# Query blocks of the attention from last to first, and the bias transposes behind the first two score blocks

## What is computed

```
q_blocks = moveaxis(q.reshape(bsz, n_blk, Q_BLOCK, MLA_HEADS, QK_HEAD), 1, 0)
def attend(args):
    qb, i = args
    q_chunk = (i * Q_BLOCK + arange(Q_BLOCK)) // CHUNK
    allowed = k_chunk[None, :] <= q_chunk[:, None]
    s = einsum("bqhd,bkhd->bhqk", qb, k) * scale
    s = where(allowed[None, None], s, neg)
    p = softmax(s, axis=-1)
    return einsum("bhqk,bkhd->bqhd", p, v)
o = lax.map(attend, (q_blocks, arange(n_blk)))
...
h = h + concatenate([conv_out, attn_out], axis=-1) @ w_o[l]
h = h + moe_ffn(rmsnorm(h, norm_ffn[l]), w_router[l], ...)
```

## Time and profile before

| | us |
|---|---|
| median of 3 runs | 2291.48 |
| lowest and highest | 2290.32 and 2299.23 |
| time of the profiled execution | 2284.88 |
| its span | 2283.0 |
| first stage, to the last transposes of queries and keys | 0 to 363.7 |
| second stage | 363.7 to 711 |
| third stage | 711 to 2283 |

### The profile page before, as it was taken

One profiled execution on the slowest core, in us unless ns is written; L12 is line 12 of the kernel. 1 busy time (PEld: TensorE's weight loads), 2 busy tenths in 40 slices (PEclk: granted clock), 3 DMA queues, 4 the chain that ended last, 5 costly groups with the idle time before them and its releaser, 6 DMA issues.

```text
span 2283.0 us, 42195 instructions
## 1 busy us (share of the span) xinstructions
PE 2123.9 (93%) x15622; PEld 1923.6 (84%) x15623; DVE 730.0 (32%) x1930; ACT 404.3 (18%) x1018; POOL 558.1 (24%) x637
## 2 busy tenths in 40 slices
PE   6999997899984899999999999999999999999992
PEld 5888885455544899999999999999999999999992
DVE  0222222333323233433233332333333333343331
ACT  1221212323211111111111111111111111111110
POOL 1122221010022223223322332222232322323321
PEclk9999998999986999999999999999999999999996
DMA  7000004212104889999998999999999989999997
GB/s 271 10 18 9 9 1 147 56 28 56 29 19 143 263 261 323 315 291 290 296 294 273 310 296 289 299 289 288 271 302 311 315 262 273 315 316 314 301 289 85
DMA packets 305781, 486.70 MB, mean 213 GB/s; under 512 B 106786, under 2 KB 128162, under 8 KB 305698
## 3 DMA queue, kind: packets, MB, share of 16 engines
q1 hardware_dynamic: 249394, 441.14, 59.2%
q0 software_dynamic: 33120, 44.91, 9.4%
q10 hardware_dynamic: 23232, 0.18, 0.6%
HBM read 454.81 MB, written 35.84 MB: 215 GB/s over the span
## 4 chain that ended last, share of the span: by engine, by line
PE 88%; DVE 3%; issue 3%; SPq 1%; ACT 1%; DMA 1%; POOL 1%; ACTq 0%; DVEq 0%; POOLq 0%
PE psum L975 41%; PE psum L991 22%; PE psum L798 7%; PE psum L940 5%; PE psum L811 2%; PE psum L889 1%; PE psum L846 1%; PE psum L814 1%; PE psum L888 1%; PE psum L923 1%; PE psum L852 1%; PE psum L906 1%; PE psum L952 1%; DMA area<-in_x 1%; DVE area L1289 1%
## 5 line engine op out<-in xcount | busy, mean ns | idle before, releaser
L975 PE MATMUL psum<-area 128*128 128x128 f32 (+2 forms) x8192 | 994.4, 284 | 40.9 <-issue 23.1
L975 PEld LDWEIGHTS psum<-area 128*128 128x128 f32 x8192 | 985.7, 192 | 46.4 <-issue 46.3
L991 PE MATMUL psum<-area 128*128 128x128 f32 (+2 forms) x4096 | 502.8, 284 | 1.6
L991 PEld LDWEIGHTS psum<-area 128*128 128x128 f32 x4096 | 491.2, 191 | 10.7 <-DVE area L1289 9.9
L1270 DVE TENSOR_SCALAR area<-psum,area 128x160 f32<-128x160 f32 x256 | 86.5, 379 | 628.5 <-PE psum L975 628.5
L575 POOL DMA_INDIRECT sum_rows<-area x165 | 261.8, 1587 | 67.3 <-issue 40.2
L737 ACT ACTIVATE area<-area 128x320 f32<-128x320 f32 x128 | 60.2, 470 | 754.2 <-DVE area L1270 754.2
L798 PEld LDWEIGHTS psum<-area 128*128 128x128 f32 x1536 | 176.2, 194 | 3.8 <-issue 3.3
L798 PE MATMUL psum<-area 128*128 128x128 f32 x1536 | 177.6, 277 | 0.0
L565 POOL DMA_INDIRECT area<-normed_rows,area x165 | 160.5, 972 | 62.1 <-issue 61.8
L560 POOL TENSOR_TENSOR area<-area 128x5 uint32<-128x5 uint32 x33 | 6.2, 189 | 644.4 <-DVE area L1255 607.1
(11 more groups left out here) (187 smaller groups left out, 1273.4 us busy)
## 6 DMA issues: line engine op xcount, KB each, us to landing
area<-in_w_gate_up SPq DMA_DIRECT2D x256, 1024.0 KB, 6.3
area<-in_w_down SPq DMA_DIRECT2D x128, 1024.0 KB, 6.9
area<-in_x SPq DMA_DIRECT2D x16, 512.0 KB, 4.0
area<-in_w_in SPq DMA_DIRECT2D x1, 4096.0 KB, 12.9
area<-in_w_o SPq DMA_DIRECT2D x1, 4096.0 KB, 13.7
sum_rows<-area SPq DMA_DIRECT2D x32, 128.0 KB, 2.7
normed_rows<-area SPq DMA_DIRECT2D x8, 512.0 KB, 2.8
out<-sum_rows SPq DMA_DIRECT2D x4, 1024.0 KB, 13.8
```

The costliest lines, as they stand in the source:

```text
L975: ins = mm(dst, w_gu[piece][:, k, c * P:(c + 1) * P], xT[:, PART * s + k, 0:width], start=(s == 0 and k == 0 and c % 2 == 0), stop=(s == 1 ...
L991: ins = mm(bank[4 + d // 3][:, (d % 3) * SLOTS:(d % 3) * SLOTS + width], w_dn[q][:, kk, d * P:(d + 1) * P], actT[:, 2 * q + kk, 0:width], ...
```

## The change

A table ORDER holds the query blocks from 7 to 0. Wherever a step used its position as the query block it now uses ORDER of the position: the length of the scores, the number of key tiles in TP and PV, the slices of queries, convolution output, x rows and of the two DRAM arrays that take h and the normalized rows. The token numbers in the constants follow the same order. The ranks inside an expert are now given from the last token block to the first, so each expert's list has its tokens in another order. The list of steps itself is the same. The order in which positions use the second transpose bank changes with the number of key tiles.

Separately, the bias transposes on TensorE and the VectorE copies behind them are moved to unit n = 2, ahead of S 2, and the wait for the copies (bank 6 is PV's output) to PV 0.

```diff
+ORDER = list(range(NT - 1, -1, -1))
...
-        "tokens": Q * (p + P * np.arange(NT, dtype=np.float32)[None, :]),
+        "tokens": Q * (p + P * np.array(ORDER, np.float32)[None, :]),
...
-            if kind == "HT" or (kind == "TP" and n // HEADS >= 4):
+            if kind == "HT" or (kind == "TP" and ORDER[n // HEADS] >= 4):
...
-                sp.dma_start(h_sb[i], x_rows[i]).then_inc(hx_in[i], 16)
+                sp.dma_start(h_sb[i], x_rows[ORDER[i]]).then_inc(hx_in[i], 16)
...
-            pe.wait_ge(bias_in, 16 * 3)
             pe.wait_ge(qT_ready, 3 * NT)
             pe.wait_ge(kT_ready, NT)
-            for c in range(2 * NC):
-                tr(bank[7][:, c * E:(c + 1) * E], bias_rows[0:E, c * P:(c + 1) * P], ident[0:E, 0:E])
...
-            pe.wait_ge(bias_ready, 2)
             pe.wait_ge(conv_done, NT)
+
+            def turn_biases():
+
+                pe.wait_ge(bias_in, 16 * 3)
+                for c in range(2 * NC):
+                    tr(bank[7][:, c * E:(c + 1) * E], bias_rows[0:E, c * P:(c + 1) * P], ident[0:E, 0:E])
...
                 if kind == "S":
-                    i, h = n // HEADS, n % HEADS
+                    i, h = ORDER[n // HEADS], n % HEADS
+                    if n == 2:
+                        turn_biases()
...
                 if kind == "PV":
-                    i, h = n // HEADS, n % HEADS
+                    i, h = ORDER[n // HEADS], n % HEADS
                     pe.wait_ge(turn_a_read, use_a[("TP", n)])
+                    if n == 0:
+                        pe.wait_ge(bias_ready, 2)
...
-                        lhs = convT[:, k, i * P:(i + 1) * P] if k < NF else attnT[:, k - NF, :]
+                        lhs = convT[:, k, ORDER[i] * P:(ORDER[i] + 1) * P] if k < NF else attnT[:, k - NF, :]
```

More of the change, by code:

```diff
@@ L443, in _ @@
             for i in range(NT):
-                b = i % 2
+                b, rows_at = i % 2, slice(ORDER[i] * P, ORDER[i] * P + P)
                 sp.wait_ge(h_ready, 2 * (i + 1))
@@ L447, in _ @@
                 for q in range(Q):
-                    sp.dma_start(acc_by_chunk[i * P:(i + 1) * P, :, q, :], h_chunks[:, :, q, :]).then_inc(h_out, 16)
+                    sp.dma_start(acc_by_chunk[rows_at, :, q, :], h_chunks[:, :, q, :]).then_inc(h_out, 16)
                 sp.wait_ge(hf_ready, i + 1)
-                sp.dma_start(hf_dram[i * P:(i + 1) * P, :], hf).then_inc(hf_out, 16)
+                sp.dma_start(hf_dram[rows_at, :], hf).then_inc(hf_out, 16)
                 if i + 2 < NT:
                     sp.wait_ge(h_out, 16 * Q * (i + 1))
-                    sp.dma_start(h_sb[b], x_rows[i + 2]).then_inc(hx_in[b], 16)
+                    sp.dma_start(h_sb[b], x_rows[ORDER[i + 2]]).then_inc(hx_in[b], 16)
             sp.wait_ge(tables_ready, 1)
@@ L681, in _ @@
                 if kind == "S":
-                    i = n // HEADS
-                    L = (i + 1) * P
+                    L = (ORDER[n // HEADS] + 1) * P
                     act.wait_ge(s_max, n + 1)
@@ L692, in _ @@
                 if kind == "TP":
-                    i = n // HEADS
+                    i = ORDER[n // HEADS]
                     act.wait_ge(turn_a, use_a[(kind, n)])
@@ L858, in _ @@
             turn_qk(NT - 1)
-            pe.wait_ge(bias_in, 16 * 3)
             pe.wait_ge(qT_ready, 3 * NT)
             pe.wait_ge(kT_ready, NT)
-            for c in range(2 * NC):
-                tr(bank[7][:, c * E:(c + 1) * E], bias_rows[0:E, c * P:(c + 1) * P], ident[0:E, 0:E])
-            for c in range(KD):
-                ins = tr(bank[6][:, c * E:(c + 1) * E], bias_rows[0:E, 2 * FF + c * P:2 * FF + (c + 1) * P], ident[0:E, 0:E])
-            ins.then_inc(bias_turned, 1)
-            pe.wait_ge(bias_ready, 2)
-            pe.wait_ge(conv_done, NT)
+            pe.wait_ge(conv_done, NT)
+            def turn_biases():
+                pe.wait_ge(bias_in, 16 * 3)
+                for c in range(2 * NC):
+                    tr(bank[7][:, c * E:(c + 1) * E], bias_rows[0:E, c * P:(c + 1) * P], ident[0:E, 0:E])
+                for c in range(KD):
+                    ins = tr(bank[6][:, c * E:(c + 1) * E], bias_rows[0:E, 2 * FF + c * P:2 * FF + (c + 1) * P], ident[0:E, 0:E])
+                ins.then_inc(bias_turned, 1)
             def rank_of(n, dst):
@@ L897, in _ @@
                         pe.wait_ge(exp_done, n + 1)
-                        src = [prob[n % 2][:, k * P:(k + 1) * P] for k in range(n // HEADS + 1)]
+                        src = [prob[n % 2][:, k * P:(k + 1) * P] for k in range(ORDER[n // HEADS] + 1)]
                     if kind == "OT":
@@ L1118, in _ @@
             nm = attn_stat[:, 120:128]
-            dve.wait_ge(bias_turned, 1)
-            V.tensor_copy(bguT, bank[7].rearrange("p (c e) -> p c e", e=E)).then_inc(bias_ready, 1)
-            V.tensor_copy(bdT, bank[6][:, 0:KD * E].rearrange("p (c e) -> p c e", e=E)).then_inc(bias_ready, 1)
-            V.memset(cums[:, 0, :], 0.0)
-            V.tensor_copy(entries[:, :, :, 0], last(K["tokens"], TOPK))
             def places(n):
@@ L1134, in _ @@
             for kind, n in steps:
+                if kind == "S" and n == 2:
+                    dve.wait_ge(bias_turned, 1)
+                    V.tensor_copy(bguT, bank[7].rearrange("p (c e) -> p c e", e=E)).then_inc(bias_ready, 1)
+                    V.tensor_copy(bdT, bank[6][:, 0:KD * E].rearrange("p (c e) -> p c e", e=E)).then_inc(bias_ready, 1)
+                    V.memset(cums[:, 0, :], 0.0)
+                    V.tensor_copy(entries[:, :, :, 0], last(K["tokens"], TOPK))
                 if kind == "S":
-                    i = n // HEADS
-                    L = (i + 1) * P
+                    L = (ORDER[n // HEADS] + 1) * P
                     sc = psum[:, (n % 2) * 1024:(n % 2) * 1024 + L]
@@ L1147, in _ @@
                     if kind == "TP":
-                        m = n // HEADS + 1 - 4
+                        m = ORDER[n // HEADS] + 1 - 4
                         if n >= 2:
```

## The result

| | before | after |
|---|---|---|
| median of the runs | 2291.92 us | 2305.06 us |
| lowest to highest (runs) | 2290.32 to 2299.23 (6) | 2301.41 to 2306.74 (6) |
| the profiled execution | 2284.88 us | 2306.74 us |
| its mean granted clock | 0.966 | 0.958 |

The ratio is 1.0051 (95% interval 1.0036 to 1.0066): the changed kernel is slower by 0.5%, 11.7 us (the two medians differ by 13.1). The forecast was +4.7. The time lies in the range, near its upper end, where the prediction gave 0.16 to being slower by more than 0.5%. The sign is the forecast's; the size is not.

What follows compares the result with a forecast made beforehand. TensorE, busy for 93% of the span, was taken to bound the kernel. The terms -6.5 + 1.4 - 1.7 + 7.2 - 0.5 + 4.8 gave +4.7 us on the median of 2291.48: 2296 us, range 2283 to 2307.

Steps and rivals of the forecast that it cites:

- S 0 earlier: Start of the second stage: the first scores start at about 364.95 instead of 371.43, -6.5 us.
- Bias transposes: Ahead of S 2: the transposes move but do not vanish, +1.4 us at full clock, +2.75 if still half.
- First position at low clock: Behind S 0's start: half-clock loss of 2.4 us instead of 4.1, so -1.7 us (between 0 and -2.4).
- Waits: Behind the odd output projections: TensorE waits longer where short units give less cover, +7.2 us in all, +5.4 from first PVs.
- second waits: At the next PV behind those projections: 1.2 us for one tile, 0.65 for two, 0.2 for three; +1.1 us.
- Small terms: HT's copy, PV 30 and the work behind the last unit: together -0.5 us.
- Clock in the short positions: Last, short positions: half-clock stretches lose 9.9 us instead of 5.1, so +4.8 us (0 to +14).
- rival B: Last three positions: clock falls early and stays low into the next projection, +17.3 us, 2309 us; chance 0.13.
- A: Short positions: clock falls no more often than before, term zero, sum -0.1, 2291 us; chance 0.27.
- C: Second stage: waits behind projections do not grow, only S 0's early start counts, -8, 2283 us; chance 0.06.
- D: Third stage: expert lists in another order change gathers and scatters, 0 with 4 us to either side; chance 0.06.

Runs made afterwards that it cites:

- e3: The changed kernel with the scores' second matmul over 128 rows instead of 64 in units 0 to 3; 2329.49 us, not comparable; S 0 to the experts 365.9 us.
- e11: The changed kernel with the scores' first matmul over 64 of its 128 rows in units 0 to 3; total not comparable, clock back 8 us behind S 0.
- e4: The changed kernel plus seven unread matmuls in TensorE's wait ahead of the last transposes; 2278.1 us, ratio 0.9939.
- e12: The kernel before, unchanged, profiled a second time; 2292.0 us.
- e10: e9 plus 1, 2, 2 and 3 unread matmuls in the waits behind the odd projections of positions 4 to 7; 2265.57 us, ratio 0.9889.
- e1: The kernel before with only the bias transposes moved to unit 2, blocks in their old order; 2283.33 us, ratio 0.9954.
- e7: The changed kernel with the loads of w_o and all behind it held until the fourth unit's exponential is done; 2302.98 us (one run).
- e5: e1 plus the seven unread matmuls ahead of the last transposes; 2281.9 us, ratio 0.9957.
- e6: The kernel before plus the seven unread matmuls ahead of the last transposes; 2283.32 us, ratio 0.9964.
- e2: The kernel before with only the block order reversed, bias transposes still ahead of S 0; 2303.81 us, ratio 1.0044.
- e8: e5 plus unread matmuls ahead of the last PV, the last position's HT, the ranks and the experts; 2266.22 us, ratio 0.9888.
- e9: e8 with the blocks from last to first and 4 instead of 3 unread matmuls ahead of PV 31; 2271.6 us, ratio 0.9924.

## Why the prediction was right or wrong

1. **S 0 earlier: right.** L785 to S 0 took 4.06 us instead of 10.57, -6.5 as forecast. It started at 363.76, not 364.95, since L785 came 1.2 earlier in that execution.
2. **Bias transposes: the other price.** They ran from 381.69 to 384.4, 2.7 us, which the prediction had named for a half clock. I took the full clock. PV 0 did not wait for the copies, as forecast.
3. **First position at low clock: wrong, and the largest miss.** The step that failed is "In the only stretch like that, the even projection behind the last unit, the clock rose 3.3 us after its start". I took a loss of 2.4 us from it, with ends of 1.7 and 4.1; it was 16.9. The projection has dense 512-column matmuls, but all over 128 rows; the scores alternate 128 and 64. (Whether that is why they differ is supported by e3 and e11, not settled.) The projection was not the only stretch to read, either: the scores of before, at 0.50 for 8.2 us, were the same matmuls but for their length, and I had no ground to make their loss the upper end. e3 and e4 confirm that this is where the time went: they take 15.6 and 15.8 us off the second stage. Against the execution of the prediction the term is +12.8; against e12 it is +5.0; the forecast had -1.7.
4. **Waits: right for the first PV; the second ones were covered by the low clock.** For 6 to 1 tiles the first waits were 0 (0.41 on VectorE instead), 0.65, 1.59, 2.13, 2.56 and 2.98: 9.9 against the 10.4 of the forecast. The second waits did not come: the PVs at 576.45, 612.93 and 643.38 start with no wait. Behind 609 and 640 the clock was at half in between, and the slower PV, TP and S covered the chain; the cost was then in the clock. At full clock, in e10, these two waits are 0.56 and 1.08, where 0.65 and 1.2 had been worked out. The wait of 0.77 that three tiles had before is gone for another reason, and ScalarE's timeline of after shows it:

```profile
575.92 0.48 ACT L698 ACTIVATE area<-psum 128x384 f32<-128x384 f32 x1
```

This copy ends at 576.40, just ahead of PV at 576.45. From the first PV to the end of the chain it is now 3.0 us, not 3.3, since ScalarE's longer copy (0.58 us instead of 0.36) lets the first PV start later while VectorE works on. And the first PV is that of a block with four tiles, 0.99 us instead of 0.55, which covers the rest. All waits of the stage are +6.5 against e12, where +7.2 was forecast.
5. **Small terms: right.** HT's group went from 2.7 to 2.4 us. PV 30 waited 0.37. From TP 31 at 669.79 to OT 7 at 675.59 are 5.8 us (forecast 6.0), with a wait of 3.62 at PV 31 (3.5 to 4).
6. **Clock in the short positions: direction right, size low.** +4.8 was forecast; +6.8 was measured against e12 and about +10 against the profiled before. In the last position the clock fell at the wait, as described, rose at 646.8, and was low again from 650.2 to 657. The falls near 473, 537 and 585 I had not counted, and three of the six (473, 585, 650) stand at a router and the projection behind it, not behind one of the long waits; and before itself varies, from three falls to four.

**The starting point** was the other miss. I saw that the profiled execution was 6.6 us below the median and put the sum on the median, which was right for what both executions have in common. But the terms 3 and 6 were taken as differences from its low clock of 8.2 us and its three falls, and these were what made it fast. With e12's figures in their place, term 3 would have been 2.4 - 11.9 = -9.5 instead of -1.7, and term 6 would have had 8.5 to subtract instead of 5.1. The same working would then have given some 6.5 us faster, not 4.7 slower. So the right sign is luck: the loss behind S 0 was taken 14.5 us too low, and the untypical base hid half of that. That the time lies in the range is luck too, since its upper end was drawn with rival B's last positions in mind and not the start.

**The rivals.** A (the clock falls no more often) is out. B had the place half right, low in the last positions, but its 17 us were not there; the time came instead at the start. C had its first term right. D is out: the third stage is 1559.6 against 1558.0 and 1558.5. What the prediction said would show in the new profile came for the terms 1, 4 (first waits) and 5; "the clock up 3 to 8 us after 365" is the line that showed the error, at 397.6.

What stays open: why e1 gained 10.5 us, and whether after's low clock of 34 us is as long in each of its executions. Its six runs lie within 5.3 us of each other and have clocks of 0.957 to 0.959, where the runs of before beside e1 to e11 have 0.959 to 0.967, and e7, with the same queue on TensorE, had 31 us; both speak for it.

## What to carry to other kernels

Profile the kernel before more than once, and look at what differs between two executions of it, before a term is taken as a difference from one of them. A moved piece of work is to be priced at the clock of the place where it lands, and a low clock is priced from the same instructions at low clock, not from the ones that look most like them. Where a wait of TensorE is followed by a long stretch of its work, a few unread matmuls in the wait can be worth more than the wait: here seven of them gave 16 us of the second stage in e4. That holds only where the clock then stays up: in e5 and e6 the same seven took about 1 us or nothing off that stage, since the clock was lost again at 366 and 364.6.

## What the runs showed that I had not expected

**A busy TensorE at half clock for 34 us.** In after the profile shows no idle time from 364 to 394, and it stayed at 1.2 GHz; in e12 it was at half clock for 24 us behind S 0, with a wait of 0.7. The Trainium skill, "TensorE: Matmul & The Clock Gate", section "What's actually happening", says that TensorE comes to its full clock when it is kept busy. e3 agrees, with 4.6 us; after, e7 and e12 do not, as far as the profile's busy time tells (the starts in e3 and e11 show that it can hide some 0.3 us in 2).

**The third stage got shorter by code that is not in it.** Its matmuls number 12288 in all of before, after, e4 and e8, and its mean clock is 0.98. It took 1558 to 1560 us in before, e12, after, e1 and e2, 1549 to 1552 in e4, e5 and e6, and 1542 to 1544 in e8, e9 and e10, which have more matmuls ahead of it. The difference is mostly in one row of the list of waits, the one where TensorE waits for nothing that the profile shows. Of e12, after, e4 and e8, each over its third stage:

```profile
PE psum L975 <- issue: 23.4, 21, 10.3
```
```profile
PE psum L982 <- issue: 23.2, 18, 10.4
```
```profile
PE psum L984 <- issue: 16.0, 14, 5.5
```
```profile
PE psum L994 <- issue: 11.3, 13, 5.5
```

The longest of these, 10 us, stands at the first tile of a width that had not run before (of before, then of e4; in brackets the idle time):

```profile
781.55 4.69 PE L975 MATMUL psum<-area 128*128 128x144 f32 x19 [9.85 <-issue]
```
```profile
777.74 10.44 PE L984 MATMUL psum<-area 128*128 128x144 f32 x68 [5.49 <-issue]
```

What it is in the added instructions that shortens these pauses no run tested, and it stays open. It means that of e4's 27 us some 7 to 11 have nothing to do with the clock, and that part of the gain of e5, e6 and e8 to e10 is of that kind: e6's almost wholly. The kernels that showed the order's effect (before, after, e1, e2) agree in this row, so the verdict on the change is not touched.
